# Mixer B: ScalarE's turned copy moved from behind the exponentials to directly behind the values copy

## The reference

```python
def nsa_attention(h, w_in, w_out, ...):          # 16 heads of 64, 4 key groups
    q, kc, vc, ks, vs, kw, vw, gate = split(h @ w_in)
    p_cmp = masked_softmax(q @ kc_b * scale)      # compressed keys, 15 of them
    o_cmp = p_cmp @ vc_b
    o_slc = selected_block_attention(q, ks, vs, sel_idx, rel_bias)
    o_win = banded_attention(q, kw, vw, rel_bias, 512)
    g = sigmoid(gate)
    o = g[..., 0:1] * o_cmp + g[..., 1:2] * o_slc + g[..., 2:3] * o_win
    return o @ w_out
```

## Time and profile before

| | |
|---|---|
| three runs | 2669.33 us median (2666.51 to 2671.46) |
| the profiled execution, its own time | 2666.94 us |
| its span in the profile | 2664.7 us |
| busy share of the span | TensorE 97%, VectorE 68%, ScalarE 54%, GpSimd 7% |
| chain of work that ended last | TensorE 86%, VectorE 5%, ScalarE 3%, DMA 2% |
| copy L1512, whole kernel | 48 of it, 812 ns median |

### The profile page before, as it was taken

How to read it: one execution, slowest core, us unless ns; L and a number is a source line. 1 busy time by engine, 2 the same in 40 slices (tenths; PEclk the granted TensorE clock), 3 DMA queues, 4 the chain that set the end, 5 groups by cost and what they waited for, 6 DMA issues and landing times.

```text
span 2664.7 us, 43984 instructions
## 1 busy us (share of the span) xinstructions
PE 2594.8 (97%) x15457; PEld 2259.9 (85%) x15457; DVE 1808.8 (68%) x2578; ACT 1449.8 (54%) x2304; POOL 189.1 (7%) x266
## 2 busy tenths in 40 slices
PE   7999999999999999999989999999999999999999
PEld 7888888888888878888888688888888888888887
DVE  6866668666766676676676666676656667666766
ACT  4655546455555565555555655555556555555654
POOL 2010001000000030000001200000010000002000
PEclk9999999999999999999999999999999999999999
DMA  6559845487566447656654266566446666653664
GB/s 188 160 171 236 226 152 159 143 238 210 170 194 189 137 148 219 190 177 195 190 175 134 88 200 190 178 196 189 151 138 194 189 205 181 199 164 129 184 191 144
DMA packets 587098, 473.78 MB, mean 178 GB/s; under 512 B 19676, under 2 KB 546416, under 8 KB 586480
## 3 DMA queue, kind: packets, MB, share of 16 engines
q1 hardware_dynamic: 582768, 457.37, 56.6%
q0 software_dynamic: 3312, 14.36, 2.4%
q10 hardware_dynamic: 912, 0.63, 0.1%
HBM read 469.09 MB, written 6.37 MB: 178 GB/s over the span
## 4 chain that ended last, share of the span: by engine, by line
PE 86%; DVE 5%; ACT 3%; DMA 2%; issue 2%; POOL 1%; DVEq 1%; SPq 0%; POOLq 0%; ACTq 0%
PE acc L784 20%; PE gu L751 14%; PE tp L751 14%; PE tp L758 7%; PE gu L758 7%; PE acc L817 3%; DVE lo_a L454 2%; ACT hi_a L442 1%; DMA raw_a<-in_w_in 1%; PE acc L1463 1%; PE gu L1421 1%; PE gu L1430 1%; PE acc L1465 1%; PE acc L1464 1%; PE gu L1422 1%
## 5 line engine op out<-in xcount | busy, mean ns | idle before, releaser
L454 DVE TENSOR_TENSOR lo_a<-raw_a,hi_a 128x2048 fp32r<-128x2048 f32 (+1 forms) x313 | 711.1, 2272 | 359.1 <-ACT hi_a L442 357.7
L442 ACT ACTIVATE hi_a<-raw_a 128x2048 fp32r<-128x2048 f32 (+1 forms) x313 | 591.5, 1890 | 125.2 <-PE acc L1465 31.7
L751 PE MATMUL tp<-xT,hi_a 128*128 128x512 f32 x1600 | 398.4, 391 | 0.0
L751 PE MATMUL gu<-xT,hi_a 128*128 128x512 f32 x1600 | 397.9, 391 | 0.0
L751 PEld LDWEIGHTS gu<-xT,hi_a 128*128 128x128 f32 x1600 | 294.0, 188 | 56.9
L751 PEld LDWEIGHTS tp<-xT,hi_a 128*128 128x128 f32 x1600 | 293.4, 188 | 56.4
L784 PE MATMUL acc<-hi_b,h_hi 128*128 128x512 f32 x760 | 298.6, 393 | 1.3 <-issue 1.2
L784 PE MATMUL acc<-lo_b,h_hi 128*128 128x512 f32 x760 | 297.9, 392 | 0.0
L784 PE MATMUL acc<-hi_b,h_lo 128*128 128x512 f32 x760 | 295.7, 389 | 0.0
L466 DVE TENSOR_TENSOR lo_b<-raw_b,hi_b 128x1024 fp32r<-128x1024 f32 x210 | 255.9, 1219 | 0.0
L843 ACT ACTIVATE arena<-arena 128x256 f32<-128x256 f32 x200 | 83.6, 418 | 279.0 <-DVE arena L906 279.0
(11 more groups left out here) (344 smaller groups left out, 4100.8 us busy)
## 6 DMA issues: line engine op xcount, KB each, us to landing
raw_a<-in_ffn_w_in SPq DMA_DIRECT2D x352, 512.0 KB, 5.8
raw_b<-in_ffn_w_out SPq DMA_DIRECT2D x176, 512.0 KB, 3.7
raw_a<-in_w_in SPq DMA_DIRECT2D x52, 512.0 KB, 4.7
raw_a<-in_w_gate SPq DMA_DIRECT2D x44, 512.0 KB, 5.6
raw_a<-in_w_up SPq DMA_DIRECT2D x44, 512.0 KB, 6.8
raw_b<-in_w_down SPq DMA_DIRECT2D x44, 512.0 KB, 4.7
raw_a<-in_w_out SPq DMA_DIRECT2D x24, 512.0 KB, 4.3
raw_a<-in_c_w_in SPq DMA_DIRECT2D x24, 512.0 KB, 4.4
```

The source lines that it names most:

```text
L442: nc.scalar.activation(a_view(hi_a, par)[:, :, 0:width], a_view(raw_a, par)[:, :, 0:width], ACT.Copy).then_inc(a_hi, 1)
L454: nc.vector.tensor_tensor(a_view(lo_a, par)[:, :, 0:width], a_view(raw_a, par)[:, :, 0:width], a_view(hi_a, par)[:, :, 0:width].bitcast(F3 ...
L751: nc.tensor.matmul(banks[:, e, :], w_hi[:, kt, e * P:(e + 1) * P], xT[:, :, kt, :], start=(kt == 0), stop=False)
```

## The change

In `b_act`, ScalarE's order for one step of mixer B, two statements change places. In odd steps the copy of the turned probabilities of unit p-29, with its wait for `o_lo`, now comes directly behind the values copy, and the exponentials of unit p-27 behind it. In even steps the copy stood at the head already.

```diff
@@ b_act, one step p
-                if scored(s, p - 1) is not None:
-                    exp_act(act, s, scored(s, p - 1))
                 if scored(s, p - 3) is not None and p % 2:
                     if p > 29:
                         act.wait_ge(o_lo, s.pair0 + (p - 31) // 2 + 1)
                     turned_act(act, s, scored(s, p - 3))
+                if scored(s, p - 1) is not None:
+                    exp_act(act, s, scored(s, p - 1))
                 ahead_b(hi_slot_a, act, s, p)
```

## The result

The changed kernel takes 2677.57 us (median of 8 runs, 2673.49 to 2679.32) against 2669.31 (8 runs, 2666.51 to 2671.66) beside it: a ratio of 1.003, 95% interval 1.0020 to 1.0039, or 5.3 to 10.4 us more. The medians are 8.3 us apart, where 7.0 was forecast. The profiled execution took 2677.52.

What follows compares the result with a forecast made beforehand. TensorE's own work was taken to bound the stretch. Entry +2.37 and ring +4.12, with the exit, put unit 14's turning at +5.7; clock +1.3 made +7.0 on 2669.33, so 2676.4 us, range 2671 to 2682.5.

Steps and rivals of the forecast that it cites:

- What bounds the kernel: Mixer B, 1463 to 1502 us: TensorE's own work bounds it, busy 38.0 of 39 us; other engines have little to spare.
- The ring: Units 7 to 15, score read to score read: pairs take 9.44 (weight copy) or 9.93 us (remainder), four pairs +4.12.
- 0.87 + 0.71 - 0.27: ScalarE, odd steps: wait for the subtraction plus turned copy, less the former gap; exponentials start 1.31 us later.
- The entry: Steps 29 and 31 onward: later exponentials delay unit 5's score read 1.97 us, unit 6's scores 1.6, unit 7's read 2.37.
- Rival C: Entry: the early copy heals unit 3's turning and its low clock, -2 us in all; chance 0.06.
- The exit: Behind unit 15's score read: unit 14's turning waits for GpSimd and comes 5.7 us later; everything behind moves in line.
- The clock: TensorE's low-clock stretches around new idle times: -1.2 to 4 us, taken as +1.3.
- upper bound: Low clock lasts through the values product at 1457, about 2 us, and another stretch at 1508, again about 2.
- both long idle times of before brought a low stretch: TensorE's waits of 2.31 and 1.82 us preceded low clock, so no less of it was counted on.
- B (slack): Middle pairs: the exponentials have slack after all, leaving only entry and exit, +0 to +3 us; chance 0.17.
- D (low clock as the rule): Five pairs with new TensorE idle times run at low clock, +22 us; chance 0.04.

Runs made afterwards that it cites:

- middle kernel: Changed kernel with the new order only from step 33 on, steps 29 and 31 as before: 2671.82 us, ratio 1.0009 to the kernel before.
- split copy: Changed kernel with the odd steps' turned-probabilities copy cut in two, 512 columns without the wait, 256 behind it: 2674.01 us, ratio 1.0014 to before.
- entry kernel: Changed kernel with the new order only in steps 29 and 31, later steps as before: 2671.72 us, ratio 1.0009 to the kernel before.

## Why the prediction was right

**What bounds the kernel.** Right. TensorE had almost no gap before, and VectorE's score read was close behind it; the changed order made that read the late one.

**The ring.** The terms 0.87 + 0.71 - 0.27 held. Pairs with a weight copy came out at 9.51 (forecast 9.44), those with a remainder at 9.91 (9.93), four pairs at 38.84 (38.74). The middle kernel has the same four with nothing changed at the entry, and the split copy shortens each by just what it takes off ScalarE's path. This is the step that the experiments settle: +4.2 us, in the profiled stage. The middle kernel's time, 1.7 to 2.4 us more with an interval of 0 to 4.8, neither confirms nor contradicts it.

**The entry.** Unit 5's score read +1.91 (1.97), unit 6's scores +1.62 (1.6), unit 3's turning -0.07 (0), its wait now ended by GpSimd. Rival C needed this turning to gain and it did not. The entry kernel shows the same numbers by itself.

**The exit.** Unit 15's read to unit 14's turning 1.83 (forecast 1.89), and waiting 1.75 (1.9). Everything behind moved in line.

**The clock, mis-sized.** I took +1.3 for it, a guess between nothing and 4; what the ring and the two ends leave of the 8.3 is about 2.5. Unit 7's score read moved by 4.19 and not by 2.37, and this 1.8 is the stretch of low clock at the entry. It had lasted through the scores and the turning only the earlier trace rows. Now it lasts 6.8 us instead of 3.4, on through the values product, which took 2.72 us instead of 1.52 and started 0.6 later than I had it. That was the first half of my upper bound ("about 2"), and it came nearly whole, in both profiles of the changed kernel. The other half, a second stretch at 1508 through the turning and values product of units 14 and 13, did not come: unit 14's turning and what follows run at full clock. The low clock at the exit stands behind unit 15's turning, as it did before. There the failed step is another one: "both long idle times of before brought a low stretch" was read from one execution. The second profile of before has none at the exit. If before has it in every second execution and the changed kernel, as in both of its profiles, always, this adds some 0.8 us. So the sum is 2.4 + 4.2 - 0.8 = 5.8 for entry, ring and exit (the 0.8: unit 14's turning stood 2.65 us behind unit 15's read and now stands 1.83 behind it), + 1.8 + 0.8 = 8.4, where the medians are 8.3 apart. The 5.8 is shown in the profiles, the 1.8 is in both of the changed kernel, and the 0.8 is argued from two against two. That the sum meets the medians to 0.1 is partly luck: the stretch behind the wait for the DMA is in both profiles of the changed kernel and in one of before, and counted in the same way it would add 0.6, which gives the 9.1 by which the stage is longer (182.9 against 173.85, means of two).

**The rivals.** B (slack) falls with the middle kernel's +4.7 at unit 14's turning, though its time of +1.7 to 2.4 us, read alone, would have spoken for B. C falls at unit 3's turning. D (low clock as the rule) falls with the window 1471 to 1513 at clock 1.00: waits of 1.01 and 1.41 us, each behind some 8.5 us of work, brought no low clock there, nor in the second profile or the middle kernel.

## What to carry to other kernels

In an engine's in-order queue, an instruction with a wait ahead of it costs its wait as well as its time to everything behind it. Put it behind the instructions that others are waiting for, if its own result is needed late: here 1.31 us in each of six steps at ScalarE and 0.7 in the first, 8.6 in all, of which TensorE covered about a third, became 5.8 us. To tell whether an engine with idle time has slack, follow the loop of handovers once around and compare its length with the busy engine's work per round, not the busy shares: they were the same before and after. And when two kernels differ by a few microseconds, take a second profile of the one before ahead of explaining the clock.

## What the runs showed of the hardware

**Two engines at SBUF.** VectorE's subtraction over 128x2048 takes 3.00 us where GpSimd's multiplications are running as it starts (six of six, and GpSimd's own 1.62 does not change). In the other 58 of the thirteen profiles, between 1430 and 1512 us, they had ended, and it takes 2.28 or 2.29. The Trainium skill, SBUF — State Buffer, section "Who interferes with whom", says that a VectorE instruction with two inputs in SBUF contends with a GpSimd instruction that reads SBUF, that the port pair they share is an exclusive lock, and that the order of issue decides which of them is blocked. The rows agree: VectorE comes second, and its 0.72 extra is near, if below, the 0.86 us that GpSimd had still to run (1477.72 + 1.62 - 1478.48). In the changed kernel the two don't meet: a remainder starting at 1483.69 follows products that end at 1483.49.

**The clock is not set by the code alone.** At the entry all thirteen profiles have TensorE wait 2.24 to 2.31 us for unit 3's turning. In ten of them the granted clock falls to 0.50 (1.2 GHz) behind it, in three it stays at 1.00. Behind the 1.82 us wait at the exit it fell in three profiles of eight, and behind the 1.73 to 1.78 us wait for a DMA at unit 1's scores in seven of thirteen. The three without a stretch at the entry are among these seven; the other four had both. With the old order at the entry a stretch there lasted 3.4 us, with the new one 6.8 (five profiles each): the second wait, 1.2 to 1.8 us at unit 6's scores, goes with a stretch twice as long. Whether it is that wait that prolongs it was not tried by itself; with the reciprocal moved, waits of 2.25 and 1.72 us close to each other brought none.
